# GpSimd adds the sublayer's output to x for the upper columns at every boundary, VectorE only for the lower 1024

## The reference, cut to what matters

```python
def rms_norm(x, gain):
    xf = x * lax.rsqrt(jnp.mean(x * x, axis=-1, keepdims=True) + NORM_EPS)
    return xf * gain

# layer 0: latent attention, then the convolutional FFN
x = x + rms_norm(mla_mixer(rms_norm(x, a_attn_norm_pre), ...), a_attn_norm_post)
x = x + rms_norm(conv_ffn(rms_norm(x, ffn_norm_pre[0]), ...), ffn_norm_post[0])
# layer 1: shared keys and values, differential attention, FFN
k1, k2, v = shared_kv(x, positions, shared_kv_norm, shared_w_kv)
x = x + rms_norm(diff_mixer(rms_norm(x, b_attn_norm_pre), ..., k1, k2, v, ...), b_attn_norm_post)
x = x + rms_norm(conv_ffn(rms_norm(x, ffn_norm_pre[1]), ...), ffn_norm_post[1])
return x
```

## Time and profile before

| | |
|---|---|
| median of 3 runs | 2221.43 us (2221.27, 2221.43, 2224.23) |
| profiled execution, its own time | 2224.47 us |
| span of the trace in it | 2222.7 us |
| busy, share of the span | PE 99%, PEld 86%, DVE 64%, ACT 55%, POOL 0% |
| mean granted TensorE clock | 0.997 of full speed |

### The profile page before, as it was taken

The page is one execution under the profiler, slowest core; times in us unless marked ns, Lnnn a source line. Parts: engine busy times, 40 slices in busy tenths (PEclk is TensorE's granted clock), DMA queues, the critical chain, the costliest instruction groups (busy, mean ns, idle before and its releaser), DMA issues.

```text
span 2222.7 us, 33628 instructions
## 1 busy us (share of the span) xinstructions
PE 2195.7 (99%) x12053; PEld 1907.4 (86%) x12053; DVE 1420.5 (64%) x1895; ACT 1224.2 (55%) x1693; POOL 3.9 (0%) x16
## 2 busy tenths in 40 slices
PE   9999999999999999999999998999999999999998
PEld 9989987888888888888878887888888888888887
DVE  6556656677677767544476667566767776774444
ACT  6655555666556655443365557455655665564443
POOL 0000000000000000000000000000000000000000
PEclk9999999999999999999999999999999999999999
DMA  8555335565656566656655652556565656566664
GB/s 280 181 178 165 111 123 175 176 205 172 206 172 202 174 205 191 209 185 203 190 182 182 197 172 75 183 161 186 172 206 171 203 174 206 171 216 201 195 191 151
DMA packets 208368, 405.58 MB, mean 182 GB/s; under 512 B 12877, under 2 KB 16327, under 8 KB 207519
## 3 DMA queue, kind: packets, MB, share of 16 engines
q1 hardware_dynamic: 207711, 400.29, 57.6%
q0 software_dynamic: 576, 4.19, 0.5%
HBM read 402.34 MB, written 2.10 MB: 182 GB/s over the span
## 4 chain that ended last, share of the span: by engine, by line
PE 97%; DVE 2%; ACT 1%; issue 0%; DMA 0%; DVEq 0%; ACTq 0%
PE ps L491 49%; PE ps L520 29%; PE ps L528 15%; PE ps L604 1%; PE ps L670 0%; PE ps L673 0%; PE ps L694 0%; DVE x L1786 0%; PE ps L666 0%; PE ps L624 0%; DVE w_lo L1439 0%; ACT probs L1180 0%; ACT w_hi L984 0%; PE ps L709 0%; PE ps L706 0%
## 5 line engine op out<-in xcount | busy, mean ns | idle before, releaser
L1445 DVE TENSOR_TENSOR w_lo<-w_raw,w_hi 128x1024 fp32r<-128x1024 f32 (+1 forms) x636 | 763.8, 1212 | 519.9 <-ACT w_hi L990 515.7
L990 ACT ACTIVATE w_hi<-w_raw 128x1024 fp32r<-128x1024 f32 (+1 forms) x636 | 658.8, 1048 | 487.4 <-PE ps L491 348.1
L520 PE MATMUL ps<-xT,w_hi 128*128 128x512 f32 x2816 | 675.1, 392 | 2.1 <-DVE xT L1823 2.1
L520 PEld LDWEIGHTS ps<-xT,w_hi 128*128 128x128 f32 x2816 | 518.1, 189 | 102.7 <-issue 2.5
L528 PEld LDWEIGHTS ps<-xT,w_lo 128*128 128x128 f32 x2816 | 362.6, 192 | 14.4 <-DVE w_lo L1445 0.4
L528 PE MATMUL ps<-xT,w_lo 128*128 128x256 f32 x2816 | 368.3, 283 | 0.0
L491 PE MATMUL ps<-w_hi,hT_hi 128*128 128x512 f32 x704 | 273.9, 389 | 0.0
L491 PE MATMUL ps<-w_lo,hT_hi 128*128 128x512 f32 x704 | 273.9, 389 | 0.0
L491 PE MATMUL ps<-w_hi,hT_lo 128*128 128x512 f32 x704 | 273.9, 389 | 0.0
L1439 DVE SCALAR_TENSOR_TENSOR w_lo<-w_raw,gcol,w_hi 128x512 fp32r<-128x512 f32 x224 | 156.3, 748 | 82.2 <-ACT w_hi L984 82.1
L491 PE MATMUL ps<-w_hi,xT 128*128 128x512 f32 x640 | 200.5, 390 | 0.0
(11 more groups left out here) (252 smaller groups left out, 2177.9 us busy)
## 6 DMA issues: line engine op xcount, KB each, us to landing
w_raw<-in_ffn_w_in SPq DMA_DIRECT2D x352, 512.0 KB, 4.2
w_raw<-in_ffn_w_out SPq DMA_DIRECT2D x176, 512.0 KB, 4.6
w_raw<-in_shared_w_kv SPq DMA_DIRECT2D x48, 512.0 KB, 3.7
w_raw<-in_a_w_o SPq DMA_DIRECT2D x32, 512.0 KB, 4.4
w_raw<-in_b_w_in SPq DMA_DIRECT2D x32, 512.0 KB, 4.6
w_raw<-in_b_w_o SPq DMA_DIRECT2D x32, 512.0 KB, 4.7
w_raw<-in_a_w_mem_kv SPq DMA_DIRECT2D x16, 512.0 KB, 7.1
w_raw<-in_b_w_mem_kv SPq DMA_DIRECT2D x16, 512.0 KB, 4.6
```

Source lines behind the costliest of these rows:

```text
L520: mm = nc.tensor.matmul(ps[:, base + m4, :].rearrange("p (a n) -> p a n", a=2), w_hi[:, slot, cols], xT[:, :, 2 * k + c, :], start=k == c ...
L990: nc.scalar.activation(w_hi[:, s % R, 0:width], w_raw[:, s % R, 0:width], ACT.Copy)\
L1445: nc.vector.tensor_tensor(w_lo[:, s % R, 0:width], w_raw[:, s % R, 0:width], w_hi[:, s % R, 0:width].bitcast(F32), ALU.subtract)\
```

## The change

At each boundary DVE keeps three pieces, the lower 1024 columns: (tile 0, 0 to 1023), (tile 1, 0 to 511), (tile 1, 512 to 1023). At OUT it keeps tile 1's 1024 to 1535 too. POOL does the others, in this order: (0, 1024 to 2047), (1, 1024 to 1535), (1, 1536 to 2047), each with two instructions: a multiplication of `y` by the inverse, in place, and an addition into `x`. It waits for the inverse (`inv_ready`), for its own multiplication (`y_scaled`), and for the last piece for `y`'s last columns (`pair_dve`), and counts `x_pool`. PE, ACT and SP wait for `x_pool` where they waited for the upper pieces; PE's wait before group 4 is for columns up to 1535 alone, with another before group 6. POOL's gain transfers stay in its queue, each now behind a boundary's pieces. The excerpt leaves out the new semaphores' declarations and the like edits for SKV on ACT.

```diff
-FFN_PIECES = ((0, 0, 1024), (0, 1024, 1536), (1, 0, 512), (1, 512, 1024), (0, 1536, 2048),
-              (1, 1024, 2048))
-SKV_PIECES = ((0, 0, 1024), (1, 0, 512), (1, 512, 1024), (0, 1024, 2048), (1, 1024, 2048))
+DVE_PIECES = ((0, 0, 1024), (1, 0, 512), (1, 512, 1024))
+POOL_PIECES = ((0, 1024, 2048), (1, 1024, 1536), (1, 1536, 2048))
...
+            stores = ((x_piece, 1, 0, 0, 1024), (x_pool, 1, 0, 1024, 2048), (x_piece, 2, 1, 0, 1024),
+                      (x_pool, 2, 1, 1536, 2048), (x_piece, 3, 1, 1024, 1536))
...
+            def pieces(no, y, tiles_done, parts=POOL_PIECES):
+
+                for k, (t, a, z) in enumerate(parts):
+                    pool.wait_ge(inv_ready, 2 * no + t + 1)
+                    if t == 1 and z == D:
+                        pool.wait_ge(pair_dve, tiles_done)
+                    scaled[0] += 1
+                    nc.gpsimd.tensor_scalar(y[:, t, a:z], y[:, t, a:z], nrm[:, 4 + t:5 + t], None,
+                                            ALU.mult).then_inc(y_scaled, 1)
+                    pool.wait_ge(y_scaled, scaled[0])
+                    nc.gpsimd.tensor_tensor(x[:, t, a:z], x[:, t, a:z], y[:, t, a:z], ALU.add)\
+                        .then_inc(x_pool, 1)
+
+            scaled = [0]
+            pieces(0, y_o, IN0_T)
+            gain("ffn_post0", gain_f, OUT0)
+            pieces(1, y_f, SKV_T)
+            gain("b_post", gain_o, SKV)
+            pieces(2, y_o, IN1_T)
+            gain("ffn_post1", gain_f, OUT1)
+            pieces(3, y_f, OUT1_T + 4, (POOL_PIECES[0], POOL_PIECES[2]))
...
                 def between(k):
-                    if k == 0:
-                        pe.wait_ge(x_piece, pieces + len(FFN_PIECES))
+                    if k in (0, 2):
+                        pe.wait_ge(x_pool, pieces + 2 + k // 2)
...
                 if part == 1 and k < LEAD:
-                    if k == 0:
-                        pe.wait_ge(x_piece, PIECES_SKV + len(SKV_PIECES))
+                    if k in (0, 2):
+                        pe.wait_ge(x_pool, PIECES_SKV + 2 + k // 2)
                     x_transpose(4 + k, range(TT)).then_inc(tr_ready, 1)
...
                 if t == half == 0:
                     act.wait_ge(x_piece, pieces)
+                    act.wait_ge(x_pool, pieces)
...
                 piece(*p[0])
                 splits_to(s_in + 2)
+                sum_last()
+                inverse_shared(1)
                 piece(*p[1])
-                sum_last()
-                inverse_std(1, 2)
                 piece(*p[2])
-                piece(*p[3])
                 last_tile()
...
-                    if g == 1:
-                        dve.wait_ge(pair_dve, t_in)
-                        piece(*p[4])
-                        piece(*p[5])
...
                 lo(2, 1)
                 lo(3, 1)
-                dve.wait_ge(pair_dve, SKV_T)
-                piece(*p[3])
-                piece(*p[4])
                 for g in range(4, DSTEPS):
```

More of the change, by code:

```diff
@@ L50 @@
 R = 4
-X_PIECES = ((0, 1024), (1024, 1536), (1536, 2048))
 HOLD = R
@@ L84 @@
 T_QPE, T_FFN0, T_KB, T_QB, T_FFN1 = 8, 11, 12, 13, 17
-FFN_PIECES = ((0, 0, 1024), (0, 1024, 1536), (1, 0, 512), (1, 512, 1024), (0, 1536, 2048),
-              (1, 1024, 2048))
-SKV_PIECES = ((0, 0, 1024), (1, 0, 512), (1, 512, 1024), (0, 1024, 2048), (1, 1024, 2048))
-PIECES_IN0, PIECES_SKV = 0, len(FFN_PIECES)
-PIECES_IN1 = PIECES_SKV + len(SKV_PIECES)
-PIECES_OUT = PIECES_IN1 + len(FFN_PIECES)
+DVE_PIECES = ((0, 0, 1024), (1, 0, 512), (1, 512, 1024))
+POOL_PIECES = ((0, 1024, 2048), (1, 1024, 1536), (1, 1536, 2048))
+PIECES_IN0, PIECES_SKV, PIECES_IN1, PIECES_OUT = 0, 3, 6, 9
 GAIN_ROWS = {}
@@ L283, in program @@
         x_piece = sem("x_piece")
+        x_pool = sem("x_pool")
+        inv_ready = sem("inv_ready")
+        y_scaled = sem("y_scaled")
         rstd_ready = sem("rstd_ready")
@@ L401, in _ @@
                              i * 1024 + 512 * j, 2 * FSTEPS, i)
[L403 to L409, removed]
+            stores = ((x_piece, 1, 0, 0, 1024), (x_pool, 1, 0, 1024, 2048), (x_piece, 2, 1, 0, 1024),
+                      (x_pool, 2, 1, 1536, 2048), (x_piece, 3, 1, 1024, 1536))
+            for semaphore, value, t, a, z in stores:
+                sp.wait_ge(semaphore, PIECES_OUT + value)
+                sp.dma_start(out[t * P:(t + 1) * P, a:z], x[:, t, a:z]).then_inc(out_stored, 16)
+            sp.wait_ge(out_stored, 16 * len(stores))
         @blk.gpsimd
@@ L434, in _, with gain @@
                 .then_inc(gain_landed, 16)
[L435 to L441, removed]
-                pool.dma_start(dst[:, :], vec[name].partition_broadcast(P)).then_inc(gain_landed, 16)
+            def gain(name, dst, step):
+                pool.wait_ge(step_used, step)
+                pool.dma_start(dst[:, :], vec[name].partition_broadcast(P)).then_inc(gain_landed, 16)
+            def pieces(no, y, tiles_done, parts=POOL_PIECES):
[17 more added lines that the diff above has]
+            pieces(3, y_f, OUT1_T + 4, (POOL_PIECES[0], POOL_PIECES[2]))
         @blk.tensor
@@ L849, in ffn_in @@
                     if g % 2 == 0:
-                        pe.wait_ge(x_piece, pieces + 3 + g // 2)
+                        pe.wait_ge(x_piece, pieces + 2 + g // 2)
                     x_transpose(g, [1]).then_inc(tr_ready, 1)
@@ L1277, in hand_over_to_ffn @@
                     if g >= 4:
-                        a = square_x((g - 4) // 2, g % 2, pieces + len(FFN_PIECES))
+                        a = square_x((g - 4) // 2, g % 2, pieces + len(DVE_PIECES))
                 a.then_inc(sq_ready, 1)
@@ L1305, in hand_over_to_skv @@
                     hi(g)
-                    a = square_x((g - 4) // 2, g % 2, PIECES_SKV + len(SKV_PIECES))
+                    a = square_x((g - 4) // 2, g % 2, PIECES_SKV + len(DVE_PIECES))
                 a.then_inc(sq_ready, 1)
@@ L1416, in _ @@
             n_split = [0]
-            count = {"N": 0, "sq": 0, "std": 0, "gain": 0, "bank": 0}
+            count = {"N": 0, "sq": 0, "std": 0, "gain": 0, "bank": 0, "inv": 0}
             def split(s, per=0, i=None):
@@ L1462, in inverse_std, with inverse_shared @@
                 link(nc.vector.reciprocal(nrm[:, 4 + t0:4 + t1], nrm[:, 2 + t0:2 + t1]))
+            def inverse_shared(t):
+                count["std"] += 1
+                count["inv"] += 1
+                dve.wait_ge(std_ready, count["std"])
+                nc.vector.reciprocal(nrm[:, 4 + t:5 + t], nrm[:, 2 + t:3 + t]).then_inc(inv_ready, 1)
+                dve.wait_ge(inv_ready, count["inv"])
             def diagonal(dst, tiles=range(TT)):
@@ L1781, in wide_epilogue @@
                 link(last_tile(0))
-                inverse_std(0, 1)
+                inverse_shared(0)
                 def piece(t, a, z):
@@ L1807, in hand_over_to_ffn @@
                 piece, sum_last, last_tile = stage
-                p = FFN_PIECES
+                p = DVE_PIECES
                 piece(*p[0])
                 splits_to(s_in + 2)
+                sum_last()
+                inverse_shared(1)
                 piece(*p[1])
-                sum_last()
-                inverse_std(1, 2)
                 piece(*p[2])
-                piece(*p[3])
                 last_tile()
@@ L1842, in hand_over_to_skv @@
                 piece, sum_last, last_tile = stage
-                p = SKV_PIECES
+                p = DVE_PIECES
                 def lo(g, t=None):
@@ L1975, in _ @@
             piece, sum_last, last_tile = wide_epilogue(OUT1, OUT1_T, FSTEPS, y_f, gain_f)
-            for a, z in X_PIECES:
-                piece(0, a, z)
+            piece(0, 0, 1024)
             sum_last()
             last_tile()
[L1980 to L1983, removed]
+            inverse_shared(1)
+            piece(1, 0, 1024)
+            piece(1, 1024, 1536)
 _INS = ["x", "mem", "positions", "a_attn_norm_pre", "a_w_in", "a_q_norm", "a_w_uq", "a_kv_norm",
```

## The result

The changed kernel takes 2231.84 us (median of 6 runs, 2231.27 to 2233.34), the kernel before 2221.51 us in the same runs (2219.93 to 2224.23). The ratio is 1.0045 with a 95% interval of [1.0035, 1.0055]: slower, by some 10 us. The forecast was 2232.5.

What follows compares the result with a forecast made beforehand. PE, busy 99% of the span, was taken as the bound, so only its waits count. Terms 4.4 + 1.4 + 1.8 + 0.7 = 8.3 us on 2224.47 gave 2232.8, stated as 2232.5; 8-in-10 range 2217 to 2239.

Steps and rivals of the forecast that it cites:

- What VectorE sheds: Pieces leaving VectorE: worth nothing on PE's path at IN0 and IN1; at SKV 2.0 us of wait, up to 1.8 of clock.
- What GpSimd gets: Per 1024 columns, a multiplication of 1.3 us and an addition of 2.2, together 3.5 us (2.2 to 4.8).
- IN0 and IN1: At these two boundaries the piece PE waits for starts 2.2 us late at each, 4.4 us in all.
- the second of the two that I gave: At IN0 VectorE keeps the path while work is queued; GpSimd's addition ends at 381.55, the piece 1.9 us late.
- a GpSimd that is only slow changes nothing: At IN0 a 512 piece has from 379.6 to past 385, three times the time given it, so slowness alone is harmless.
- The first way: At IN0 GpSimd's instructions alternate with VectorE's; last sum only at 381.6, the piece 2.7 us late, 3.3 with a multiplication.
- The clock at IN0 and IN1: Longer gaps before PE's product slow TensorE's clock: 0 to 2.8 us more, middle 1.4.
- SKV: First low half delayed 2.0 us, a 512 piece among splits adds 1.85, PE's wait of 2.0 goes: +1.8 us.
- the clock stays as it was: At SKV the 1.8 us of slow clock in the profiled execution remains, since PE has more and earlier gaps.
- OUT: Last pieces end 1.1 us later, part hidden under stores already queued: +0.7 us.
- Rival (b): Side by side, nothing slowed: SKV's wait of 2.0 us and clock loss of 1.8 go, 2217.6 us; chance 25%.
- (c): GpSimd yields, working in VectorE's pauses while VectorE keeps its times: 2218 to 2225, about 2221 us; chance 15%.

Runs made afterwards that it cites:

- skv_only: GpSimd's pieces at SKV alone, all else as in the kernel before; 2222.83 us against 2222.84, ratio 1.0005.
- out_only: GpSimd's pieces at OUT alone, all else as in the kernel before; 2223.81 us against 2222.84, ratio 1.0007.
- skv_order: Kernel before, no GpSimd pieces; at SKV one upper piece moved into VectorE's pause, the other cut in two with a finer PE wait; 2219.63 us against 2221.91.
- skv_out: As skv_order, plus OUT's tile 1 lower piece and store cut in two and a wait moved later; 2220.28 us against 2222.49 for the kernel before.
- add_later: Changed kernel, but GpSimd's first addition at IN0 and IN1 waits for VectorE's three pieces; 2228.89 us against 2221.91 for the kernel before.
- in_only: GpSimd's pieces at IN0 and IN1 alone, all else as in the kernel before; 2228.26 us against 2222.84, ratio 1.0027.
- unscaled: Changed kernel without GpSimd's multiplication at all four boundaries, upper columns getting y unscaled; 2229.77 us against 2221.91 for the kernel before.
- add_256: Changed kernel with every GpSimd addition cut into instructions of 256 columns; 2228.95 us against 2221.91 for the kernel before.

## Why the prediction was right, point by point

The forecast, its direction and its main mechanism held: where both read SBUF, VectorE and GpSimd's addition go one at a time. For the multiplication "a whole instruction" was too much: VectorE waited 0.84 us at most for its 2.84. By its own terms:

**What VectorE sheds** was not quite nothing at IN0 and IN1: the splits grew by 0.83 us and ACT's wait hid only 0.24 of it, so without the piece that had gone from ahead of it the last sum would have come about 0.6 us later (an estimate from these two). At SKV the wait of 2.0 us before group 4 went.

**What GpSimd gets.** The addition was 2.35 us where I took 2.2. The multiplication is the term that was mis-sized: 2.84 us for 1024 columns and 1.56 for 512, where I took 1.3 and bounded it by 1.6, from the slope of a select over 128 columns. The Trainium skill, GPSIMD Engine Reference, section 3.1, agrees with the addition (4497 ns for 2048 columns) and not with the multiplication, for which, by its nearly one cycle per column, an estimate for 1024 would be 0.9 us; the measurement decides.

**IN0 and IN1**, 2.2 us of wait each: measured from the last sum to the product's start, 6.24 less 3.90, 2.34, at IN0, and 2.30 at IN1. The size is right and the way is the second of the two that I gave (the addition ending at 381.55; it ended at 381.59), yet that agreement is luck. The addition started that late because the multiplication is long and grew beside VectorE's work (2.84 us alone, 4.98 here), not because GpSimd had to wait for VectorE's pause. With a multiplication of 1.3 us it would probably have met a split, as it does in the run that leaves the multiplication out. I had also said that a GpSimd that is only slow changes nothing; its slowness is what put the addition, by 0.03 us, ahead of the piece that PE waits for. The first way, a late last sum, is what happened once the multiplication was taken out.

**The clock at IN0 and IN1**, 1.4 us: +1.54 at IN0, whose first eight matmuls now took 3.63 us in place of 2.09, and -0.48 at IN1, where it had been slow before. Together 1.1.

**SKV**, +1.8 us: measured -0.48, and +1.1 at equal clock. The delay itself was near: PE's first step of part 1 came 16.80 us after the sum (at 1130.47 by PE's timeline) in place of 13.46 (1123.58), +3.3 where I had 3.85. It lies elsewhere than I put it: the first low half isn't late at all (5.08 us after the sum, 5.06 before), and the splits behind it are, since the addition lies there. What failed is the step that the clock stays as it was. I had taken the slow clock of the one profiled execution (1.8 us, of which 0.2 are no clock: the first transposes behind a wait take 0.66 us at full clock too) for SKV's own. It is not: of the three kept executions with this SKV unchanged one has it. That the changed kernel lacks it can't be put down to its gaps having moved ahead, since two of the three with the old gaps lack it as well.

**OUT**, +0.7 us: measured +2.39. It is the multiplication again: GpSimd ended tile 0 at 2222.59, 1.1 us after tile 1's inverse (2221.44), and its last two instructions, 2.52 and 1.26 us, came on top.

The terms made 8.3 us and the spans differ by 7.3: two errors of near 2 us, at SKV and OUT, cancelled, and that is luck too. Rival (b), side by side, is ruled out by the pair measured alone. Against (c), GpSimd yields, speak VectorE's own instructions, which did not keep their times (3.95 us in place of 1.42), and PE's waits, none of which is for a piece of GpSimd's. Two of the signs that I had named for the forecast came only in part: the last sum at IN0 started 0.04 us after ACT's, not 2, and PE's waits there are 3.9 us at IN0 and 4.3 at IN1, where I had asked for over 4 at each.

The kept traces also tell how regular the clock is at IN0 and IN1. Where the product starts 3.9 us after the last sum (the six kept runs without an addition ahead of the critical pieces there: the kernel before, `skv_only`, `out_only`, `skv_order`, `skv_out`, `add_later`), its first eight matmuls ran at a lowered clock in 4 of 12 stretches. Where it starts 4.6 to 6.2 us after (the changed kernel, `in_only`, `unscaled`, `add_256`), they did in 8 of 8, at a granted 0.50 to 0.53. So the longer gap brings the slow stretch along nearly always here, and that fits the changed kernel's narrow spread (2.1 us in 6 runs, before 4.3).

## What to carry to other kernels

Before handing an idle GpSimd part of VectorE's elementwise work, look at what VectorE does at that moment: if it reads two operands from SBUF, the two take turns, and one GpSimd addition placed just ahead of the instruction that everybody waits for costs nearly its own length. Short instructions lessen that, at the price of more GpSimd time; moving it only changed the victim here. Look first for a pause of VectorE's own and for a wait that asks for more than it needs: here a piece in a 1.47 us pause and a finer wait gave 1.7 us at the very place where GpSimd's help cost 1.1. And before a slow stretch of the one profiled execution is put into a forecast, look whether another execution has it.

## What was not expected of the hardware

GpSimd's multiplication by a per-partition scalar, with one input, is slower than its addition of two: 2.84 against 2.35 us for 1024 columns, and 2.77 with a constant in place of the scalar. And the two hold VectorE up differently: an addition for up to 2.15 us, nearly its length, a multiplication for 0.84 us at most here, while it itself grows by 1.4 to 2.1. Why the multiplication lets VectorE in between is open.
